# Seeding the expert sums with x, and a differently ordered loop of expert pairs, in a two-layer encoder trunk

## The chip, the cores and the metric

The kernel runs on one core of a Trainium2 chip. The metric is the device time in microseconds (us), as the median over runs; lower is better. The engines are TensorE (PE in the profile; PEld is its weight loads), VectorE (DVE), ScalarE (ACT), GpSimd (POOL) and SyncE (SP), which here issues nearly all DMA transfers.

## The reference, cut to what matters

The input x has 256 tokens of 1024 channels. There are two layers, each a mixer followed by a mixture of experts; the end is an RMS norm. The change touches only the mixture's sum and the end.

```python
def hier_moe(...):            # 4 groups of 8 experts; top-1 group, top-2 experts in it
    ...
    hg = jnp.einsum('sd,edf->sef', t, w_gate)      # 32 experts, 1024 -> 256
    hu = jnp.einsum('sd,edf->sef', t, w_up)
    act = jax.nn.silu(hg) * hu * combine[:, :, None]
    return jnp.einsum('sef,efd->sd', act, w_down)  # 256 -> 1024

for i in range(2):
    x = x + g_m * mixer_i(modulate(rmsnorm(x)))
    x = x + g_f * hier_moe(modulate(rmsnorm(x)))
return rmsnorm(x, norm_out)
```

All data are float32. The weights of 32 experts in each of two layers (3 MB an expert) are most of what is read from memory.

## The kernel before, in words

Each engine has its own program, and semaphores order them. The work around the change is `experts(l)`, which exists once for each engine, for layer l = 0 and 1.

**Pairs of experts.** The kernel routes the 512 token copies (256 tokens, two experts each) so that the copies of one expert stand together, and takes the experts two at a time: 16 pairs p = 0 to 15 in a layer. Each expert has a window of 64 slots; the two windows of a pair make the 128 rows of one tile. Two pairs make a group, `group(i)`, with b = p % 2 naming the buffer of a pair. (With badly unbalanced routing there would be more groups; the number is read from a register, and is 8 here.)

**TensorE, for pair p:** `gate_half` (32 matmuls, L983), `up_half` (L995), `turn_act` (two transposes of the activations, L1003), and then `down` of the pair *before* it, p - 1 (L1016). `combine(p - 2)` (L1042) multiplies the result of pair p - 2 by a 0/1 matrix `sel` and so adds each slot's row to its token's row: eight matmuls, on four PSUM banks (bank 4 and 5 for the first 512 columns of the two token tiles, 6 and 7 for the second). The result is carried as a high and a low float32r part, hence `part`. The banks 4 to 7 gather the sum over all pairs of a layer.

**Where combine stands before the change:** for p = 2 and 3 behind `up_half`; from p = 4 on between `gate_half` and `up_half`. Groups 0 and 1 are written out, and the loop `Fori(2, groups)` does the rest. The very first matmuls on the banks (p = 0) start the sum with start=True. After the loop come `down_last` (L1028) for pair 15 and the combines of the pairs 14 and 15, the last of which raise `mix_done`.

**VectorE, for pair p:** `silu_mul` (the product that turns gate and up into the activation, L1776 and L1781), `places` (L1788 to L1795: it builds `sel` for pair p, and waits for the semaphore `comb_done`, since combine(p - 2) reads the same buffer), `keep_y(p - 1)` (L1806 evacuates `down`, L1811 makes the low part). **ScalarE:** the windows of the next pair, tanh, the copy of the turned activations, and the high part (`high_y`, L1310). Both have loops of their own, which start at group 2.

**SyncE** issues the weight loads in one order of its own, in one queue: gate(p), up(p) (2 MB each, L348 and L352), and down (2 MB, L356 and L361). gate(p) waits for `gate_done` of pair p - 2, up(p) for `unit_done` of pair p - 2 (the last matmul of `up_half`), down for `down_done`. So a transfer can be issued when TensorE has finished with the slot two pairs before, and not earlier; a wait holds all that is behind it in this program. The last down weights come as four transfers of 0.5 MB (L431).

**After the experts:** `combined(l)` on VectorE adds the four banks to x_res (L1849), in the order first half, both tiles, second half, both tiles; ScalarE squares what has been added (`squares`, L1139) with a running sum; VectorE turns the sums into mean squares (`mean_square`, L1381 and L1383) and GpSimd takes the power -1/2 (`power`, L474). At the very end this is spread over two tiles: VectorE multiplies x by the norm's gain (L1876), GpSimd takes two powers (L550), ScalarE scales tile 0 (L1362), VectorE does tile 1 in one instruction of 1024 columns (L1880), and SyncE stores the tiles (L446) as each is done.

## Time and profile before

| | |
|---|---|
| time, median of 3 runs | 685.51 us (684.13 to 686.7) |
| time of the profiled execution | 686.04 us |
| span of the profiled execution | 684.3 us |
| PE busy | 628.0 us (92%) |
| DVE busy | 358.6 us (52%) |
| ACT busy | 179.4 us (26%) |
| read from memory | 268.17 MB, 393 GB/s over the span |

A span is shorter than its execution's time by what lies around it, 1.7 us here. Busy times are sums over stages with different limits: TensorE at 92% and the queue of weight loads (96.6% of the 16 DMA engines' span) both look full, and which of them sets the time has to be read stage by stage. A row of the timeline has its start, its length, engine and line, the operation with its tiles, how many instructions were merged (x32), and in brackets the idle time before it with what ended it.

### The profile page before, as it was taken

How to read it: one execution, taken by the hardware profiler on the slowest of the kernel's cores; microseconds unless marked ns; L12 is line 12 of the kernel's file. 1: busy time of each engine (PE TensorE's matmuls, PEld its weight loads, DVE VectorE, ACT ScalarE, POOL GpSimd, SP SyncE). 2: the span in 40 equal slices, each digit the busy share in tenths (PEclk: the TensorE clock that was granted, in tenths of full speed). 3: DMA queues.
4: the chain of work that ended last, by engine and by line, in shares of the span. 5: the costliest groups of instructions: out<-in, count | busy, mean ns of one | idle time of the engine just before them, and what ended most of it. 6: DMA issues, size and time to landing. Idle time of an engine off the chain costs nothing.

```text
span 684.3 us, 11449 instructions
## 1 busy us (share of the span) xinstructions
PE 628.0 (92%) x4226; PEld 378.8 (55%) x4226; DVE 358.6 (52%) x869; ACT 179.4 (26%) x370; POOL 62.3 (9%) x111
## 2 busy tenths in 40 slices
PE   2799999998999999999998989999999999999894
PEld 1597758446766455545554457666555544555442
DVE  2257988998454643344334465735444344433445
ACT  2123252013431222122212233342223122221213
POOL 5010408950000000000000000000000000000000
PEclk9899999999999999999999999999999999999998
DMA  8999967999999999999999999999999999999991
GB/s 326 367 399 394 381 249 269 400 417 417 383 410 418 422 420 422 421 423 422 423 421 421 408 399 411 420 420 422 421 420 420 422 421 421 422 421 423 422 375 65
DMA packets 51534, 269.63 MB, mean 394 GB/s; under 512 B 4112, under 2 KB 6224, under 8 KB 27440
## 3 DMA queue, kind: packets, MB, share of 16 engines
q1 hardware_dynamic: 50720, 268.22, 96.6%
q0 software_dynamic: 784, 1.01, 0.5%
q8 instruction: 19, 0.31, 0.2%
q14 instruction: 11, 0.09, 0.0%
HBM read 268.17 MB, written 1.05 MB: 393 GB/s over the span
## 4 chain that ended last, share of the span: by engine, by line
PE 75%; DMA 17%; DVE 5%; issue 1%; SPq 0%; ACT 0%; POOL 0%; DVEq 0%; POOLq 0%
PE bank L983 15%; PE bank L995 14%; PE bank L1016 12%; DMA ring<-in_w_gate 11%; PE bank L1042 7%; DMA ring<-in_w_mod 6%; PE bank L860 4%; PE bank L699 4%; PE bank L948 2%; PE bank L783 2%; PE bank L793 2%; DVE hT L1781 2%; PE bank L612 2%; PE bank L1003 1%; PE bank L729 1%
## 5 line engine op out<-in xcount | busy, mean ns | idle before, releaser
L983 PE MATMUL bank<-ring,arena 128*64 128x256 f32 x1024 | 116.9, 380 | 3.5 <-DMA ring<-in_w_gate 3.5
L995 PE MATMUL bank<-ring,arena 128*64 128x256 f32 x1024 | 117.2, 381 | 0.0
L983 PEld LDWEIGHTS bank<-ring,arena 128*64 128x64 f32 x1024 | 75.6, 137 | 51.8 <-issue 21.6
L995 PEld LDWEIGHTS bank<-ring,arena 128*64 128x64 f32 x1024 | 72.3, 137 | 41.1 <-issue 8.6
L1781 DVE SCALAR_TENSOR_TENSOR hT<-hT,bank 128x256 f32<-128x256 f32 x32 | 19.2, 602 | 136.6 <-PE bank L995 136.6
L1310 ACT CAST xn_parts<-arena 128x512 fp32r<-128x512 f32 x64 | 39.6, 619 | 106.8 <-DVE arena L1806 106.8
L1806 DVE SCALAR_TENSOR_TENSOR arena<-bank,hT,gates 128x512 f32<-128x512 f32 x64 | 48.0, 750 | 36.7 <-PE bank L1016 35.4
L1042 PE MATMUL bank<-xn_parts,sel 128*128 128x512 f32 x256 | 67.1, 405 | 0.0
L1016 PE MATMUL bank<-dn_w,hT 128*64 128x512 f32 x256 | 58.5, 598 | 1.1 <-ACT gates L1120 1.1
L1042 PEld LDWEIGHTS bank<-xn_parts,sel 128*128 128x128 f32 x256 | 45.7, 188 | 20.9 <-issue 12.4
L1016 PE MATMUL bank<-xn,arena 128*64 128x512 f32 x112 | 51.1, 598 | 0.0
L1016 PE MATMUL bank<-gates,arena 128*64 128x512 f32 x112 | 51.1, 598 | 0.0
L1776 DVE SCALAR_TENSOR_TENSOR hT<-hT,bank 128x256 f32<-128x256 f32 x32 | 13.5, 421 | 64.1 <-ACT hT L1297 64.0
L1811 DVE TENSOR_TENSOR xn_parts<-arena,xn_parts 128x512 fp32r<-128x512 f32 x64 | 44.0, 687 | 2.8
L1290 ACT COPY arena<-arena 128x512 f32 x64 | 39.9, 623 | 9.6 <-issue 6.1
L1016 PEld LDWEIGHTS bank<-dn_w,hT 128*64 128x64 f32 x256 | 17.3, 136 | 30.9 <-issue 30.9
L612 PE MATMUL bank<-ring,cs 128*32 128x256 f32 x288 | 19.6, 421 | 14.6 <-DMA ring<-in_w_mod 14.6
L1003 PE MATMUL bank<-ident,hT 128*128 128x128 f32 x64 | 13.7, 295 | 19.3 <-DVE hT L1781 19.3
L1463 DVE SCALAR_TENSOR_TENSOR gates<-ring,cs,gates 128x1024 f32<-128x1024 f32 x23 | 30.1, 1308 | 0.8
L1301 ACT COPY hT<-bank 128x256 f32<-128x256 f32 x16 | 6.0, 372 | 92.6 <-PE bank L1003 92.6
L1301 ACT COPY arena<-bank 128x256 f32<-128x256 f32 x16 | 6.0, 373 | 88.1 <-PE bank L1003 88.1
L1016 PEld LDWEIGHTS bank<-xn,arena 128*64 128x64 f32 x112 | 14.2, 136 | 26.3 <-issue 26.3
(326 smaller groups left out, 768.0 us busy)
## 6 DMA issues: line engine op xcount, KB each, us to landing
ring<-in_w_gate SPq DMA_DIRECT2D x32, 2048.0 KB, 18.3
ring<-in_w_up SPq DMA_DIRECT2D x32, 2048.0 KB, 18.8
ring<-in_w_mod SPq DMA_DIRECT2D x20, 2048.0 KB, 17.5
dn_w<-in_w_down SPq DMA_DIRECT2D x16, 2048.0 KB, 18.3
xn<-in_w_down SPq DMA_DIRECT2D x14, 1024.0 KB, 16.9
gates<-in_w_down SPq DMA_DIRECT2D x14, 1024.0 KB, 19.8
ring<-in_w_in SPq DMA_DIRECT2D x2, 2048.0 KB, 22.0
dn_w<-in_w_mod SPq DMA_DIRECT2D x2, 2048.0 KB, 12.0
```

Source lines behind the costliest of these rows:

```text
L612: ins = pe.matmul(quadrant(vec, q), cs[:, 2, k:k + 1].to_broadcast([P, 32]), by_quadrant(w[:, kk, :], q, natural), start=not last and kk = ...
L699: ins = pe.matmul(bank[banks[m // 2]][:, (m % 2) * T:(m % 2 + 1) * T], w[:, k, m * P:(m + 1) * P], hT[:, k, :], start=(k == 0), stop=(k == ...
L983: ins = pe.matmul(bank[2][h * WIN:(h + 1) * WIN, 0:FE], xw[:, b, h, k, :], w[:, h, 0, k, :], start=(k == 0), stop=(k == KT - 1))
L995: ins = pe.matmul(bank[3][h * WIN:(h + 1) * WIN, 0:FE], xw[:, b, h, k, :], w[:, h, 1, k, :], start=(k == 0), stop=(k == KT - 1))
L1016: ins = pe.matmul(bank[n][h * WIN:(h + 1) * WIN, :], actT[b][:, t, h * WIN:(h + 1) * WIN], w[h][:, t, n * HALF:(n + 1) * HALF], start=(t = ...
L1042: ins = pe.matmul(bank[4 + 2 * n + t][:, :], sel[:, b, t * P:(t + 1) * P], xn_parts[:, part, b, n * HALF:(n + 1) * HALF], start=(isinstanc ...
L1290: ins = act.copy(xw[:, b, h], xgT[:, :, bass.ds(start, WIN)])
L1310: act.copy(xn_parts[:, 0, b, at], y_s[:, b, at]).then_inc(e["y_hi"], 1)
L1463: ins = stt(acc, w, cs[:, 2, k:k + 1], acc, ALU.mult, ALU.add)
L1781: stt(act_s.rearrange("s t p -> s p t"), gl.rearrange("s (p t) -> s p t", t=FT), 0.5, bank[3][:, 0:FE].rearrange("s (p t) -> s p t", t=FT) ...
L1806: stt(y_s[:, b, at], bank[n][:, :], slot_gate[:, b:b + 1], gates[:, 2 * l + 1, at], ALU.mult, ALU.mult).then_inc(e["y_kept"], 1)
L1811: tt(xn_parts[:, 1, b, at], y_s[:, b, at], xn_parts[:, 0, b, at].bitcast(F32), ALU.subtract).then_inc(e["y_lo"], 1)
```

## The change: what it does

- `start_with_x()`, new: behind group 0, TensorE multiplies the identity by x_res (float32), four products of 128x512, with start=True on the banks 4 to 7. So the expert sums begin with x, and no matmul of combine has start=True any more.
- `combine` takes a list of halves. For every pair from p = 2 on, the first half (banks 4 and 5) stands between `gate_half` and `up_half`, the second (banks 6 and 7) between `up_half` and `turn_act`. `comb_done` comes with the second.
- TensorE's loop starts at group 1. The loops of the other engines are as before.
- `combined(0)` copies the banks to x_res where it added them. `combined(1)` is gone.
- At the end ScalarE squares the banks themselves, once `mix_done` says that each is complete; VectorE multiplies the first halves (banks 4, 5) by the gain after the square of the same bank, then `mean_square(4)`, one `power(4)` for both tiles; VectorE finishes the second halves from the banks 6, 7, ScalarE scales the first halves, and SyncE stores tile t when both halves are done.

```diff
@@ SyncE, the stores
             for t in range(TT):
-                sp.wait_ge(*((S["x_scaled"], 3), (S["out_dve"], 1))[t])
+                sp.wait_ge(S["out_act"], t + 1)
+                sp.wait_ge(S["out_dve"], t + 1)
@@ GpSimd
-            for t in range(TT):
-                pool.wait_ge(S["mean_sq"], 5 + t)
-                pool.tensor_tensor(stat[:, 4 + t:5 + t], stat[:, 2 + t:3 + t], mhalf[:, 0:1], ALU.pow).then_inc(S["inv_rms"], 1)
+            power(4)
@@ TensorE, experts
-                def combine(p, b, last=False):
-
-                    if isinstance(p, int) and p == 0:
-                        pe.wait_ge(S["rows_act"], l + 1)
-                        pe.wait_ge(S["rows_dve"], l + 1)
+                def start_with_x():
+
+                    pe.wait_ge(S["rows_act"], l + 1)
+                    pe.wait_ge(S["rows_dve"], l + 1)
+                    for half in range(2):
+                        for t in range(TT):
+                            pe.matmul(bank[4 + 2 * half + t][:, :], ident[:], x_res[:, t, half * HALF:(half + 1) * HALF], start=True, stop=False)
+
+                def combine(p, b, halves=(0, 1), last=False):
+
                     pe.wait_ge(e["sel_kept"], p + 1)
-                    for n in range(2):
+                    for n in halves:
                         pe.wait_ge(e["y_lo"], p * 2 + (n + 1))
...
-                                                start=(isinstance(p, int) and p == 0 and part == 0), stop=(last and part == 1))
+                                                start=False, stop=(last and part == 1))
                             if last:
                                 ins.then_inc(S["mix_done"], 1)
-                    if not last:
+                    if not last and n == 1:
                         ins.then_inc(e["comb_done"], 1)
@@ group(i)
                         gate_half(p, b, i * 16 + 16)
-                        if n == XS:
-                            combine(p - 2, b)
+                        if n >= 2:
+                            combine(p - 2, b, (0,))
                         up_half(p, b, i * 16 + 16)
+                        if n >= 2:
+                            combine(p - 2, b, (1,))
...
-                        if 2 <= n < XS:
-                            combine(p - 2, b)
                         turn_act(p)
...
                 group(0)
-                group(1)
-                with pe.Fori(2, groups) as i:
+                start_with_x()
+                with pe.Fori(1, groups) as i:
                     group(i)
@@ ScalarE, squares and the end
                         else:
-                            act.wait_ge(S["x_ready" if half else "x_half"], TT * (n - 1) + t + 1)
+                            act.wait_ge(S["mix_done"], 10 + 2 * half + t + 1)
...
+                        x_now = x_res[:, t, at] if n < 4 else bank[4 + 2 * half + t][:, :]
...
-            act.wait_ge(S["x_scaled"], 2)
             act.wait_ge(S["inv_rms"], 5)
-            act.activation(xn[:, 0, :], xn[:, 0, :], ACT.Identity, scale=stat[:, 4:5]).then_inc(S["x_scaled"], 1)
+            for t in range(TT):
+                act.wait_ge(S["x_scaled"], t + 1)
+                act.activation(xn[:, t, 0:HALF], xn[:, t, 0:HALF], ACT.Identity, scale=stat[:, 4 + t:5 + t]).then_inc(S["out_act"], 1)
@@ VectorE, combined and the end
-                    ins = tt(x_res[:, t, at], x_res[:, t, at], bank[4 + i][:, :], ALU.add)
+                    ins = dve.tensor_copy(x_res[:, t, at], bank[4 + i][:, :])
...
-            combined(1)
-            dve.wait_ge(S["square_sum"], 2 * TT * 4 + TT)
-            done(ts(stat[:, 0:2], stat[:, 20:22], 1.0 / D, EPS, ALU.mult, ALU.add))
             dve.wait_ge(S["row_kept"], 2)
             for t in range(TT):
-                at = slice(t * HALF, (t + 1) * HALF)
-                tt(xn[:, 0, at], x_res[:, 0, at], gates[:, 0, at], ALU.mult).then_inc(S["x_scaled"], 1)
-                dve.wait_ge(S["square_sum"], 2 * TT * 4 + TT + t + 1)
-                stt(stat[:, 2 + t:3 + t], stat[:, 22 + t:23 + t], 1.0 / D, stat[:, t:t + 1], ALU.mult, ALU.add).then_inc(S["mean_sq"], 1)
-            dve.wait_ge(S["inv_rms"], 6)
-            stt(xn[:, 1, :], x_res[:, 1, :], stat[:, 5:6], gates[:, 0, :], ALU.mult, ALU.mult).then_inc(S["out_dve"], 1)
+                dve.wait_ge(S["square_sum"], 2 * TT * 4 + t + 1)
+                tt(xn[:, t, 0:HALF], bank[4 + t][:, :], gates[:, 0, 0:HALF], ALU.mult).then_inc(S["x_scaled"], 1)
+            mean_square(4)
+            dve.wait_ge(S["inv_rms"], 5)
+            for t in range(TT):
+                stt(xn[:, t, HALF:D], bank[6 + t][:, :], stat[:, 4 + t:5 + t], gates[:, 0, HALF:D], ALU.mult, ALU.mult).then_inc(S["out_dve"], 1)
```

## Rows read from the trace of the kernel before

**Rows 1.** The page, part 2: rate of all transfers in 40 slices of 17.1 us.

```profile
GB/s 326 367 399 394 381 249 269 400 417 417 383 410 418 422 420 422 421 423 422 423 421 421 408 399 411 420 420 422 421 420 420 422 421 421 422 421 423 422 375 65
```

**Rows 2.** TensorE's timeline: start us, length us, what; gate of pair 15, both layers.

```profile
379.82 3.67 PE L983 MATMUL bank<-ring,arena 128*64 128x256 f32 x32 [0.81 <-DMA ring<-in_w_gate]
...
654.04 3.67 PE L983 MATMUL bank<-ring,arena 128*64 128x256 f32 x32 [0.81 <-DMA ring<-in_w_gate]
```

**Rows 3.** TensorE's timeline: pair 9 of layer 1, in the loop.

```profile
567.73 3.62 PE L983 MATMUL bank<-ring,arena 128*64 128x256 f32 x32
571.28 2.11 PE L1042 MATMUL bank<-xn_parts,sel 128*128 128x512 f32 x8
573.32 3.67 PE L995 MATMUL bank<-ring,arena 128*64 128x256 f32 x32
577.76 0.44 PE L1003 MATMUL bank<-ident,hT 128*128 128x128 f32 x2 [0.76 <-DVE hT L1781]
...
581.61 3.62 PE L983 MATMUL bank<-ring,arena 128*64 128x256 f32 x32
```

**Rows 4.** TensorE's timeline: gates of pairs 3 and 4, layer 0.

```profile
212.87 3.62 PE L983 MATMUL bank<-ring,arena 128*64 128x256 f32 x32
...
225.64 3.62 PE L983 MATMUL bank<-ring,arena 128*64 128x256 f32 x32
```

**Rows 5.** TensorE's timeline: two float32 products of 128x512.

```profile
193.97 1.88 PE L629 MATMUL bank<-gates,ones 128*128 128x512 f32 x4
```

**Rows 6.** SyncE's timeline: issues of single 2 MB weight loads.

```profile
180.46 0.38 SPq L348 DMA_DIRECT2D ring<-in_w_gate  x1
...
203.91 0.40 SPq L348 DMA_DIRECT2D ring<-in_w_gate  x1
...
476.58 0.40 SPq L348 DMA_DIRECT2D ring<-in_w_gate  x1
...
633.56 0.38 SPq L352 DMA_DIRECT2D ring<-in_w_up  x1
638.50 0.37 SPq L356 DMA_DIRECT2D dn_w<-in_w_down  x1
```

**Rows 7.** DMA view, one issue each, order of rows 6: last column us to landing.

```profile
ring<-in_w_gate SPq DMA_DIRECT2D x1, 2048.0 KB, 7.7
...
ring<-in_w_gate SPq DMA_DIRECT2D x1, 2048.0 KB, 11.7
...
ring<-in_w_gate SPq DMA_DIRECT2D x1, 2048.0 KB, 11.9
...
ring<-in_w_up SPq DMA_DIRECT2D x1, 2048.0 KB, 25.2
...
dn_w<-in_w_down SPq DMA_DIRECT2D x1, 2048.0 KB, 25.3
```

**Rows 8.** Windows of 5 us: last columns granted clock, DMA share, GB/s.

```profile
180.00:185.00 5.00, 4.79 (x46) 2.65 (x42) 1.02 (x2) 0.99 (x3) 0.00 (x0) 1.00 0.84 283
```

**Rows 9.** DMA view of 200 to 204 us: queue, packets, MB, share of 16.

```profile
q8 instruction: 1, 0.02, 1.7%
```

**Rows 10.** Timeline of the end, all engines.

```profile
664.49 3.65 PE L1016 MATMUL bank<-dn_w,hT 128*64 128x512 f32 x16
...
674.13 2.48 DVE L1849 TENSOR_TENSOR x_res<-x_res,bank 128x512 f32<-128x512 f32 x4 [0.37 <-PE bank L1042]
...
676.71 0.61 ACT L1139 ACTIVATE arena<-x_res 128x512 f32<-128x512 f32 x1
...
679.18 1.28 DVE L1880 SCALAR_TENSOR_TENSOR xn<-x_res,stat,gates 128x1024 f32<-128x1024 f32 x1 [0.89 <-POOL stat L550]
679.89 0.96 SPq L446 DMA_DIRECT2D out<-xn  x2
```

**Rows 11.** Timeline behind layer 0: last square to the first user of the power.

```profile
403.01 0.19 ACT L1139 ACTIVATION_READ_ACCUMULATOR arena<-x_res 128x1 f32 x1
...
404.28 1.42 DVE L1390 TENSOR_SCALAR xn<-x_res,stat 128x1024 f32<-128x1024 f32 x2 [0.81 <-POOL stat L474]
```

More of the change, by code:

```diff
@@ L279, in trunk @@
             slot_ready sel_ready rows_turned rows_act rows_dve xg_done xg_act xg_dve xw_half win_ready
-            row_done row_kept band_ready x_scaled out_dve out_stored scale_ready dve_own pool_own""".split()
+            row_done row_kept band_ready x_scaled out_act out_dve out_stored scale_ready dve_own pool_own""".split()
         S = {n: sem(n) for n in names}
@@ L1135, in squares @@
                             act.wait_ge(S["x_in"], 16 * TT)
+                        elif n < 4:
+                            act.wait_ge(S["x_ready" if half else "x_half"], TT * (n - 1) + t + 1)
                         else:
-                            act.wait_ge(S["x_ready" if half else "x_half"], TT * (n - 1) + t + 1)
+                            act.wait_ge(S["mix_done"], 10 + 2 * half + t + 1)
                         at = slice(half * HALF, (half + 1) * HALF)
-                        act.activation(ar((9216 if n else 0) + t * D + half * HALF, HALF), x_res[:, t, at], ACT.Square,
+                        x_now = x_res[:, t, at] if n < 4 else bank[4 + 2 * half + t][:, :]
+                        act.activation(ar((9216 if n else 0) + t * D + half * HALF, HALF), x_now, ACT.Square,
                                        accum_out=stat[:, 20 + 2 * half + t:21 + 2 * half + t]).then_inc(S["square_sum"], 1)
```

## The prediction, made before the changed kernel was run

> **What bounds the kernel now.** I read the page's rates first. From the tenth slice on, through both loops, the transfers run at 417 to 423 GB/s nearly without a break [rows 1]; that is a full queue, and the reader is to see that it does not dip where the loops run. Then TensorE's timeline. In the middle of a layer it never waits for a transfer: a pair in the loop takes 13.88 us (567.73 to 581.61) and its only idle time is 0.76 us ahead of the transposes, where VectorE's product is awaited [rows 3]. A pair needs 6 MB of weights, three transfers of 2,097 KB, which at 421 GB/s take 4.98 us each, 14.9 a pair. So TensorE is faster than its weights by 1.06 us a pair, and eats up the lead that it got while the layer was being routed. Late in each layer the lead is gone: the gates of the last pairs (14 and 15 in layer 0, 13 to 15 in layer 1) wait for their transfer, 0.81 us at the gate of pair 15 in both layers [rows 2]. So the time at which pair 15 can start is that of a landing, and it is the end of a queue that has run without a gap since the layer's beginning. Both engines look full, but the queue binds: what TensorE saves in the loop, it will wait for at the end of the loop. What counts is (a) whether the landings move, and (b) the path from the last gate's landing, just ahead of 654.04, to the end of the span, 684.3.
>
> **The change, part by part.** *x opens the sums:* four float32 products of 128x512. Two take 1.88 us with their drain [rows 5], four some 3.5, once in each layer, behind group 0. They delay everything of pair 2 and 3 on TensorE by 3.5 us. *The loop:* the pairs 2 and 3 had their combine behind `up_half` already, and pair 3 takes 12.77 us (212.87 to 225.64) against 13.88 [rows 4, 3]: eight matmuls behind `up_half` hide VectorE's product. Now half of them stand there, 2.04 / 2 = 1.0 us (the whole takes 571.28 to 573.32), against an idle time of 0.76: covered, with 0.25 to spare. Splitting it adds two changes between the two kinds of matmul; no row has their price alone. I take 0.17 for both, an estimate between 0 and 0.3 (gate's 32 matmuls take 3.55 us ahead of combine, so little is lost at the change there [rows 3]), so 12.95 us a pair. That is 0.93 us less for each of the 12 pairs of the loop, 11 a layer, of which the x products take 3.5, and the queue takes the rest: TensorE now meets the landings from about pair 11 or 12 on and waits 2.0 us at each. `comb_done` comes half a combine later, so `places` starts some 0.5 us later; behind it on VectorE stands `keep_y(p - 1)`, and this stands as it does in pair 3 now, where TensorE shows no wait: nothing. *The loop from group 1 on:* no instruction more; pairs at the loop's turn take as long as the others; nothing, except the fetch of instructions, below. *`combined(0)`:* a copy for an add of the same tile, and ahead of a TensorE that waits for weights there: nothing.
>
> **(a) Do the landings move?** gate(4) is issued when the gate of pair 2 is done, so 3.5 us later: 207.4 for 203.91 in layer 0, 480.1 for 476.58 in layer 1 [rows 6]. There the queue is at its shortest. The price of a late issue is bounded from both sides. In layer 0 gate(2) was issued at 180.46 to a queue that had just run dry: it landed 7.7 us later, and the window around it fell to 283 GB/s, (419 - 283) / 419 x 5 = 1.6 us of the queue's time [rows 6 to 8]. By the landing: 207.4 + 7.7 = 215.1 is no later than the 203.91 + 11.7 = 215.6 of now, and in layer 1 480.1 + 7.7 = 487.8 against 488.5 [rows 6, 7]. So gate(4) has 0.5 and 0.7 us of slack even if it meets an empty queue; up(4), issued 4.6 us later than now, is still issued over 3 us before gate(4) lands. That bound says 0. By the rate: the total rate would dip in both places as it did at 180, at most 1.6 us each, 3.2 in all. The two disagree since a landing is that of the slowest of 16 engines: gate(4) needs 11.7 us though the queue ahead of it holds little more than one transfer, so one engine lags behind the mean, and the others' dip costs nothing. Below zero: an instruction fetch holds one engine for 1.7% of 16 x 4 us = 1.1 us [rows 9], and TensorE's program is shorter by one group in each layer; a fetch fewer on the lagging engine brings the landings forward by 1.1 us a layer at most, 2.2 in all. I take 0, the landings' own bound, and keep +3.2 and -2.2 for the range.
>
> The Trainium skill (DMA: Bandwidth & Descriptors, "Why a DMA increments its semaphore by 16 and not by 1") says that the engines of a transfer finish independently and only the full 16 means that all has landed. By that rule the landing's bound counts, and not the mean rate's; the trace agrees in that gate(4) of layer 0 takes 11.7 us behind a short queue [rows 7]. The same page ("Anatomy of one DMA") fits a transfer by 2.0 us plus its bytes at 436 GB/s, for another issuing path; by that 2 MB take an estimated 6.8 us where the row has 7.7, gate(4) would land at 214.2, and the sum would still be 0.
>
> **(b) The end.** Now the down of pair 14 starts at 664.49 [rows 10], 10.45 us behind the gate of pair 15 [rows 2]. In the new order that is 12.95 less down (577.76 to 581.61 less 0.36 of transposes, 3.49 [rows 3]), 9.5, so 663.5 if no weights are late. But up(15) landed at 633.56 + 25.2 = 658.8 and down(14) at 638.50 + 25.3 = 663.8 [rows 6, 7]; I allow 0.25 from a landing to the first matmul, an estimate. So `up_half` starts at 659.05 for 658.7, down at 664.1. TensorE gains 0.4 us, not 0.9; what is late next is the weights again. From there to the last product nothing changes, so VectorE's first add of now, at 674.13, is at 673.7 only a semaphore.
>
> Then: four squares of 0.61 from the banks, the first at 673.75 instead of 0.7 behind an add; the last starts at 675.6 and, with its accumulator read, ends at 676.3. Now the last starts at 676.71 and ends at 677.4 [rows 10]. VectorE's two products (about 0.7 each) lie between the squares. From the end of the last square to the first user of the power behind layer 0 it is 403.20 to 404.28, 1.08 us, with one power for both tiles [rows 11]: the last stage starts at 677.4. Now it starts at 679.18, since two powers run one after the other [rows 10]. Two products of 512 columns instead of one of 1024 columns, 0.75 and then 0.7 (1.28 now): done at 678.1 and 678.85, against 680.46. The stores: now the first is issued at 679.89 and the second right behind VectorE's end, and the span ends 3.84 behind that end; the first store is ready at 678.15 and doesn't hold the second. 678.85 + 3.84 = 682.7: the end gains 1.6 us, 0.4 of it on TensorE. Where the skipped add lets the squares start, the banks' readers are ordered one behind the other; if ScalarE reads a bank slower than x_res, at most 0.1 a square, it costs 0.4; if `up_half` were not held by its landing, it gains 0.5 more.
>
> **Sum.** Landings 0, end -1.6: the profiled execution goes from 686.04 to 684.4, span 682.7. This execution stood 0.5 above the median of its kernel, so 684.1 between the two.
>
> **Rivals.**
> *The late issues cost the queue (slower):* the fourth gate transfer of each layer, issued 3.5 us later, meets a dry queue, and the dip passes on to every landing behind it: 2 x 1.6 - 1.6 = +1.6, 687.6. For it: the rate fell to 283 GB/s in the like case [rows 8], and nothing later in a layer can give it back. Against: the landing's slack of 0.5 and 0.7 us. It turns into a slower kernel when the two dips cost over 1.6 together.
> *Fewer fetches (faster):* the queue's slowest engine is spared one instruction fetch in each layer; 2.2 + 1.6 = 3.8 less, 682.2. For it: the program is shorter, and a fetch stands in the stretch of the late landings [rows 9]. Against: in layer 0 gate(4) can't land before 215.1, which leaves 0.5 to gain there.
> *TensorE's saving shows:* 2 x (11 - 3.5) = 15 less, near 670. For it: TensorE is the busier engine and stands on most of the chain. Against: the waits for weights at pair 15 in both layers [rows 2]; for it the queue would have to be faster than 421 GB/s, which no slice shows [rows 1].
> *The half doesn't cover:* the transposes still wait. It would show in a pair over 13.2 us, and cost nothing but the 0.4 at the end: 684.8, since the queue binds.
>
> **Numbers.** Forecast (with the fourth rival, which can't be told from it in the time) 0.68, late issues 0.17, fewer fetches 0.13, TensorE's saving 0.02. Range 682.0 to 687.6: it reaches to both neighbours. Half a per cent, about what a measurement can tell from no change here, is 3.4 us: faster means below 682.1. Of the fewer fetches nearly all but the full case stays above that, so faster 0.09; slower, above 688.9, needs dips over twice as dear as the rows have them, 0.04; within 0.87.
>
> **What would show it.** Right: gate of pair 15 starts within 1 us of 379.8 and 654.0, waiting about 2 us for its transfer, in both layers; waits of that kind from pair 11 or 12 on; a pair in between of 12.9 to 13.0 us with no idle time ahead of L1003; 8 instructions of 3.5 us behind group 0; up of pair 15 held by its landing; span's end some 28.7 us behind the last gate for 30.3. Wrong: gates of pair 15 later by over 1 us with a dip near 207 or 480 (late issues), or earlier by over 1 (fetches); pairs without waits at a layer's end (TensorE's saving); or an end that doesn't shrink, say for a slower read of the banks.

## The result, and the profile after

The changed kernel takes 687.63 us (median of 17 runs, 684.93 to 693.97), the kernel before 684.55 beside it (17 runs, 683.51 to 687.47). The ratio is 1.0052, 95% interval 1.0034 to 1.0070: slower by about 3 us. The forecast was 684.1, a small gain.

The profiled execution of after took 685.28 us (span 683.5), 2.3 below the median of its kernel, so it can show only part of the loss. Its span is even 0.8 shorter than that of before, since layer 0's loads start 1.6 us earlier in it (gate(2) is issued at 178.87 for 180.46 [rows 6]), ahead of anything that the change touches. So stretches are compared, each from its own start, and a second profile of the same kernel (e1 below, 687.55 us, at its median) stands beside it.

The page of after, part 2 (rate of all transfers, 40 slices) and part 3 (queues: packets, MB, share of 16 engines):

```profile
GB/s 329 366 394 394 375 298 256 413 417 417 382 415 347 425 421 422 422 422 422 422 422 422 409 399 410 420 419 420 364 424 421 422 421 421 422 422 422 422 413 117
...
q1 hardware_dynamic: 50720, 268.22, 97.0%
...
q8 instruction: 16, 0.26, 0.2%
```

Where [rows 1] run level, two slices now dip, the 13th (418 before, 347 after) and the 29th (421 before, 364 after). They are the places of gate(4), the load of the gate weights of pair 4, in the two layers.

Windows of 5 us, two of before and then those of after (last columns: granted clock, DMA share, GB/s):

```profile
203.00:208.00 5.00, 5.00 (x44) 3.72 (x41) 1.04 (x2) 0.38 (x1) 0.00 (x0) 1.00 0.99 392
480.00:485.00 5.00, 5.00 (x24) 2.52 (x25) 3.40 (x9) 0.50 (x2) 0.00 (x0) 1.00 1.01 416
...
203.00:208.00 5.00, 5.00 (x42) 3.08 (x40) 0.42 (x1) 0.38 (x1) 0.00 (x0) 1.00 0.76 269
208.00:213.00 5.00, 5.00 (x38) 2.92 (x36) 1.77 (x5) 0.37 (x1) 0.00 (x0) 1.00 0.98 395
213.00:218.00 5.00, 5.00 (x37) 2.44 (x34) 3.74 (x8) 1.90 (x4) 0.00 (x0) 1.00 0.99 374
480.00:485.00 5.00, 5.00 (x42) 3.06 (x40) 0.42 (x1) 0.38 (x1) 0.00 (x0) 1.00 0.83 310
```

The first dip in windows of 1 us of after:

```profile
205.00:206.00 1.00, 1.00 (x11) 0.47 (x8) 0.00 (x0) 0.03 (x1) 0.00 (x0) 1.00 0.69 279
206.00:207.00 1.00, 1.00 (x6) 0.55 (x6) 0.42 (x1) 0.35 (x1) 0.00 (x0) 1.00 0.17 74
207.00:208.00 1.00, 1.00 (x11) 0.71 (x12) 0.00 (x0) 0.00 (x0) 0.00 (x0) 1.00 0.95 156
208.00:209.00 1.00, 1.00 (x14) 0.64 (x12) 0.00 (x0) 0.00 (x0) 0.00 (x0) 1.00 0.88 295
```

SyncE's timeline of after, around pair 4 (issues; layer 0, then layer 1):

```profile
178.87 0.38 SPq L348 DMA_DIRECT2D ring<-in_w_gate  x1
...
206.12 0.41 SPq L348 DMA_DIRECT2D ring<-in_w_gate  x1
210.69 0.38 SPq L352 DMA_DIRECT2D ring<-in_w_up  x1
...
481.48 0.41 SPq L348 DMA_DIRECT2D ring<-in_w_gate  x1
```

DMA view of after, one issue each: gate(4), up(4) of layer 0, gate(4) of layer 1; last column is us from issue to landing:

```profile
ring<-in_w_gate SPq DMA_DIRECT2D x1, 2048.0 KB, 8.1
...
ring<-in_w_up SPq DMA_DIRECT2D x1, 2048.0 KB, 10.9
...
ring<-in_w_gate SPq DMA_DIRECT2D x1, 2048.0 KB, 8.0
```

From gate(2)'s issue to gate(4)'s it is 27.25 us now (206.12 - 178.87), 23.45 before [rows 6]: 3.8 later. gate(4) takes 8.1 us to land for 11.7 [rows 7], which is close to what a transfer takes on a queue that has run dry (7.7). up(4) lands at 210.69 + 10.9 = 221.6, which is 7.4 us behind gate(4) and not the 5.0 of a full queue. The same up(4) in before, its issue and its DMA view:

```profile
207.21 0.38 SPq L352 DMA_DIRECT2D ring<-in_w_up  x1
...
ring<-in_w_up SPq DMA_DIRECT2D x1, 2048.0 KB, 13.3
```

TensorE's timeline of after: the products of x, a pair, and the gates of pairs 12 and 15 (layer 0), pair 15 (layer 1):

```profile
198.62 3.70 PE L1037 MATMUL bank<-x_res,ident 128*128 128x512 f32 x8
202.25 3.67 PE L982 MATMUL bank<-ring,arena 128*64 128x256 f32 x32
...
228.53 3.62 PE L982 MATMUL bank<-ring,arena 128*64 128x256 f32 x32
232.08 1.20 PE L1046 MATMUL bank<-xn_parts,sel 128*128 128x512 f32 x4
233.21 3.67 PE L994 MATMUL bank<-ring,arena 128*64 128x256 f32 x32
236.81 1.21 PE L1046 MATMUL bank<-xn_parts,sel 128*128 128x512 f32 x4
237.86 0.38 PE L1002 MATMUL bank<-ident,hT 128*128 128x128 f32 x2
...
241.66 3.62 PE L982 MATMUL bank<-ring,arena 128*64 128x256 f32 x32
...
336.14 3.67 PE L982 MATMUL bank<-ring,arena 128*64 128x256 f32 x32 [1.47 <-DMA ring<-in_w_gate]
...
380.83 3.67 PE L982 MATMUL bank<-ring,arena 128*64 128x256 f32 x32 [1.43 <-DMA ring<-in_w_gate]
...
655.29 3.67 PE L982 MATMUL bank<-ring,arena 128*64 128x256 f32 x32 [1.44 <-DMA ring<-in_w_gate]
```

A pair takes 13.13 us (228.53 to 241.66) with nothing idle ahead of the transposes, and in layer 0 five gates (pairs 11 to 15) and in layer 1 four (12 to 15) wait for their weights. TensorE has become faster than its weights by what was forecast; only the weights come later. From gate(2)'s issue to the start of pair 15, layer 0 takes 380.83 - 178.87 = 201.96 us for 379.82 - 180.46 = 199.36 [rows 2, 6]: 2.6 later.

The end of after, all engines:

```profile
674.82 0.60 ACT L1146 ACTIVATE arena<-bank 128x512 f32<-128x512 f32 x1 [1.08 <-PE bank L1046]
...
677.02 0.22 ACT L1146 ACTIVATION_READ_ACCUMULATOR arena<-bank 128x1 f32 x1
...
677.59 0.69 POOL L475 TENSOR_TENSOR stat<-stat,mhalf 128x2 f32<-128x2 f32 x1 [248.98 <-DVE stat L1391]
...
678.32 1.41 DVE L1885 SCALAR_TENSOR_TENSOR xn<-bank,stat,gates 128x512 f32<-128x512 f32 x2 [0.80 <-POOL stat L475]
679.14 1.02 SPq L447 DMA_DIRECT2D out<-xn  x2
```

From the start of pair 15 it is 683.5 - 655.29 = 28.2 us to the span's end, for 30.3 before [rows 2]: the end gained 2.0.

### The profile page after: what moved, and what is told of

Same layout as the page of the kernel before. It is cut to its first block, busy times and chain, and to the rows that moved or that the text cites. A ratio compares the mean times of both kernels' runs of the same rounds, so it can differ in the third digit from the quotient of the medians.

```text
span 683.5 us, 11501 instructions
## 1 busy us (share of the span) xinstructions
PE 636.9 (93%) x4242; PEld 378.4 (55%) x4242; DVE 358.5 (52%) x865; ACT 179.2 (26%) x371; POOL 62.8 (9%) x110
## 4 chain that ended last, share of the span: by engine, by line
PE 43%; issue 37%; DMA 17%; DVE 2%; SPq 0%; ACT 0%; POOLq 0%; DVEq 0%; POOL 0%
DMA ring<-in_w_gate 11%; PE bank L982 7%; DMA ring<-in_w_mod 6%; PE bank L994 5%; PE bank L1015 4%; PE bank L859 4%; PE bank L698 4%; PE bank L1046 2%; PE bank L782 2%; PE bank L792 2%; PE bank L611 2%; PE bank L947 1%; PE bank L1103 1%; PE bank L745 1%; PE bank L728 1%
## 5 line engine op out<-in xcount | busy, mean ns | idle before, releaser
L982 PE MATMUL bank<-ring,arena 128*64 128x256 f32 x1024 | 117.1, 380 | 12.1 <-DMA ring<-in_w_gate 12.1
L1046 PE MATMUL bank<-xn_parts,sel 128*128 128x512 f32 x256 | 75.1, 419 | 0.0
L1046 PEld LDWEIGHTS bank<-xn_parts,sel 128*128 128x128 f32 x256 | 43.5, 188 | 29.4 <-issue 23.2
L475 POOL TENSOR_TENSOR stat<-stat,mhalf 128x2 f32<-128x2 f32 x5 | 3.5, 702 | 531.4 <-DVE stat L1391 531.4
## 6 DMA issues: line engine op xcount, KB each, us to landing
dn_w<-in_w_mod SPq DMA_DIRECT2D x2, 2048.0 KB, 11.7
```

What stands on the lines that cost most here:

```text
L982: ins = pe.matmul(bank[2][h * WIN:(h + 1) * WIN, 0:FE], xw[:, b, h, k, :], w[:, h, 0, k, :], start=(k == 0), stop=(k == KT - 1))
L1046: ins = pe.matmul(bank[4 + 2 * n + t][:, :], sel[:, b, t * P:(t + 1) * P], xn_parts[:, part, b, n * HALF:(n + 1) * HALF], start=False, sto ...
```

## The experiments

Times are medians with the range. Each set has its own runs of the kernel before: 685.25 us for e1 to e4, 685.92 for e5 to e8, 685.81 for e9 to e11, 684.96 for e12. For the traces one table serves all, three stretches read from TensorE's and SyncE's timelines as above: in layer 0 from gate(2)'s issue to the start of pair 15; and from the products with the second half of the weights that layer 1's mixer waits for (L600, L601 before) to gate(2)'s issue in layer 1, and to the start of pair 15 in layer 1.

```
kernel (profiled execution)       layer 0    to gate(2)   layer 1
before                            199.36     47.85        248.78
after                             201.96     47.84        248.90
e1  after again                   201.01     49.48        250.28
e2  x behind the gate of pair 2   200.92     50.21        251.07
e4  before's order of combine     201.72     48.64        250.37
e6  after, filled middle          201.63     48.64        250.15
e5  x in pair 3                   199.25     50.14        248.74
e11 e5 again                      199.49     50.29        248.84
e7  e5, filled middle             199.30     47.84        248.14
e12 e5, idle products in pair 5   199.61     50.26        249.90
e8  split order alone             198.21     50.11        248.56
e9  before, idle x ahead          201.69     47.84        249.56
e10 before, idle x behind up      201.37     48.54        249.92
```

One execution's row is good to about a microsecond: e8's layer 0 reads 1.2 us under before's, though its kernel issues nothing earlier behind gate(2).

**e1: the changed kernel again.**

> The changed kernel itself, to see the spread of its runs and their granted clocks side by side. Theory 1 (clock): TensorE now waits for weights at the gates of the last four or five pairs of each layer, and in some runs its clock is lowered to half in that stretch; the time then goes up as the mean granted clock goes down: runs from 685 (clock 0.998) to 693 (0.982), median near 687.5, while the kernel before stays within 3 us at 684.5. Theory 2 (late issues): gate(4) of each layer comes late and every run pays the same, some 1.5 to 3 us net; then the runs would lie together and the clock would not matter.

687.6 us (685.41 to 694.18, 12 runs), ratio 1.0039 (1.0016 to 1.0063): the loss holds. Windows of its trace:

```profile
203.00:208.00 5.00, 5.00 (x38) 2.88 (x36) 0.42 (x1) 0.38 (x1) 0.00 (x0) 1.00 0.84 326
208.00:213.00 5.00, 5.00 (x39) 3.16 (x38) 0.68 (x2) 0.00 (x0) 0.00 (x0) 1.00 0.97 331
480.00:485.00 5.00, 5.00 (x39) 3.04 (x40) 0.42 (x1) 0.38 (x1) 0.00 (x0) 1.00 0.80 326
485.00:490.00 5.00, 5.00 (x40) 3.21 (x40) 0.90 (x3) 0.10 (x1) 0.00 (x0) 1.00 1.00 357
```

The same dips, and layer 1 is late here too, by 1.5 us (250.28). Of the two theories the expectation names, the mean clock (0.983 to 0.995) does go with the time here, and the late issues are in the trace; the runs of e1 alone don't part them.

**e2: the products behind the gate of pair 2**, so that gate(4) need not wait for them.

```diff
                         gate_half(p, b, i * 16 + 16)
+                        if n == 2:
+                            start_with_x()
...
-                start_with_x()
-                with pe.Fori(1, groups) as i:
+                group(1)
+                with pe.Fori(2, groups) as i:
```

> The four x products stand behind the gate matmuls of pair 2 in place of ahead of them (so pairs 2 and 3 are written out again), so gate(4) is issued as early as in the kernel before. Theory 2 (late issues): the dip of the transfer rate near 207 and 480 us goes, the lowest run falls by 1.5 to 3 us against the changed kernel's, to about 682.5. Theory 1 (clock): the lowest falls by that too if the dips cost anything, but the waits at the last gates get no shorter, so the upper runs stay 5 us and more above the lowest and the median stays above the lowest by 2 us or more.

688.27 us (685.64 to 690.11), ratio 1.0034 (1.0017 to 1.0051): nothing gained, and the lowest run is 685.64, not the 682.5 that both theories expected. gate(4) was issued at 204.87, but up(4), whose wait is for the last matmul of `up_half`, 8.0 us later at 212.88; the dips stood at 213 to 223 (297 and 333 GB/s). The late issue had only been moved from one transfer to the next; my expectation looked at gate(4) alone.

**e3: idle products in each pair of the loop**, three of 128x256 in float32 ahead of the wait for the gate's weights, whose result nothing reads: is it TensorE's idle time, with the clock behind it, that costs?

```diff
                         pe.wait_ge(e["gl_ready"], p)
+                        if not isinstance(p, int):
+                            for _ in range(3):
+                                pe.matmul(bank[2][:, FE:2 * FE], ident[:], slot_no[:, 0:FE], start=True, stop=True)
+                        pe.wait_ge(gate_in[l][b], loaded)
```

> In each pair from 2 on, three idle float32 products of 128x256 (1.3 us in all, result not used) stand ahead of the wait for the gate's weights. TensorE does more work and waits less. Theory 1 (clock): the spread goes, every run has a granted clock of 0.99 or more, and the median falls to 685 to 686, under the changed kernel's although 30 x 1.3 = 39 us of work is added. Theory 2: the median stays at 687.5; and if TensorE were the bound it would rise by up to 39 us.

714.85 us (714.09 to 715.04), ratio 1.0421 (1.0395 to 1.0446). TensorE's timeline, a pair of its layer 1:

```profile
580.29 1.56 PE L979 MATMUL bank<-slot_no,ident 128*128 128x256 f32 x6
581.78 3.67 PE L986 MATMUL bank<-ring,arena 128*64 128x256 f32 x32
```

The filler took 1.56 us a pair, in 14 pairs of each layer, and a pair 14.77. That is 21.8 us a layer, and TensorE's waits for gate weights in after, which could hide it, are 12.1 us in both layers together (its page). The experiment was ill-sized and says nothing on the clock.

**e4: the order of the combines as before**, x and the end as after; the loop starts at group 2 again.

```diff
-                        if n >= 2:
-                            combine(p - 2, b, (0,))
+                        if n == XS:
+                            combine(p - 2, b)
                         up_half(p, b, i * 16 + 16)
-                        if n >= 2:
-                            combine(p - 2, b, (1,))
...
+                        if 2 <= n < XS:
+                            combine(p - 2, b)
```

> Combine stands as in the kernel before (whole, behind up for pairs 2 and 3, ahead of up from pair 4 on), the loop starts at group 2; x products and the end on the banks as in the changed kernel. Theory 1 (clock): a pair takes 13.9 us again, TensorE reaches the landings only at pair 13 or so and the waits are 0.8 us: no spread, every clock 0.99, median 684.5 + (1.5 to 3 of late issues) - 1.2 of the end = 685 to 686. Theory 2: the same median as the changed kernel less the 0.4 that the split gives at the end, so 688.

686.15 us (685.67 to 689.69), ratio 1.0012 (0.9995 to 1.0029). The dips are there without the new order (270 GB/s at 203 to 208, 324 at 480 to 485). The time is the one expected by the clock theory (685 to 686) and not the 688 of the late issues. But no gate of a pair 15 waits for weights: with pairs as slow as before's, the 3.7 us of products make TensorE itself the bound, so its time can't be set beside after's term by term.

**e5: the products of x in pair 3.** Pair 0's combine starts the sums again; x is added in pair 3 behind its combine, behind everything that releases gate and up of the pairs 4 and 5. The loop starts at group 2, as it does in e2; everything else is the changed kernel.

```diff
-                def start_with_x():
+                def add_x():
...                          start=False, stop=False)
                             combine(p - 2, b, (1,))
+                        if n == 3:
+                            add_x()
...
-                start_with_x()
-                with pe.Fori(1, groups) as i:
+                group(1)
+                with pe.Fori(2, groups) as i:
```

> The changed kernel, but combine of pair 0 starts the sums and the four x products are added in pair 3, behind its combine; so no gate or up transfer is issued late while the queue is short, only down(6), where it is longer. Theory 2 (late issues): the dips near 206 and 482 us (269 and 310 GB/s) go, gate of pair 15 of layer 0 comes 199 to 200 us behind the issue of gate(2) as before, for 201 to 202; the lowest run falls by 1.5 to 2.5 us to about 683, the median by as much. Theory 1 (clock): the wait for the second w_mod weights between the layers stays at 2.2 us and more, so the clock is still lowered there in part of the runs and the median stays 2 us or more above the lowest.

683.16 us (681.64 to 684.50, 12 runs), ratio 0.9967 (0.9954 to 0.9980). It beats the kernel before and, by the ratios, the changed one by 0.7%. Windows of its trace:

```profile
203.00:208.00 5.00, 5.00 (x40) 2.88 (x36) 0.42 (x1) 0.38 (x1) 0.00 (x0) 1.00 0.98 378
208.00:213.00 5.00, 5.00 (x26) 2.25 (x26) 3.47 (x9) 0.99 (x2) 0.00 (x0) 1.00 1.02 429
...
475.00:480.00 5.00, 5.00 (x42) 3.43 (x40) 2.24 (x4) 2.42 (x5) 0.00 (x0) 1.00 0.99 369
480.00:485.00 5.00, 5.00 (x38) 2.96 (x36) 1.50 (x4) 0.37 (x1) 0.00 (x0) 1.00 1.01 416
...
490.00:495.00 5.00, 5.00 (x42) 3.02 (x38) 0.45 (x2) 0.95 (x2) 0.00 (x0) 1.00 1.02 429
```

The two dips are gone (a window of layer 1, 475 to 480, still reads 369 for 419 before, and pair 15 there is not late), and layer 0 is back at 199.25. So the whole loss goes with the place where the change put the products; in pair 3 no cost of them can be told. e2 has the same loop and the same work and keeps the loss, so it isn't the loop's start.

**e6 and e7: a filled wait between the layers.** Three idle float32 products of 128x512 ahead of the wait for the mixer's weights, in the changed kernel (e6) and in e5 (e7): does the loss come from a TensorE that idles there and then runs at the lower clock?

```diff
                     key = halves(vec)[part]
+                    if vec == (1, 2) and part == 1:
+                        for _ in range(3):
+                            pe.matmul(bank[2][:, :], ident[:], slot_no[:], start=True, stop=True)
                     arrived(key)
```

> The changed kernel with three idle float32 products of 128x512 (2.6 us, result not used) ahead of the one wait for weights between the layers (2.3 us in the changed kernel's profile, 3.0 us in its rerun, where the 16 matmuls behind it took 3.58 us in place of 1.92, at half clock). Theory 1: no half clock behind it any more, the mean granted clock rises from 0.990 to 0.993 or more, median 686 or less, time no longer rising to 694. Theory 2: same as the changed kernel, 687.5.

> Both edits: x products in pair 3, and the idle products ahead of the wait between the layers. If the two causes are separate the gains add: median 683.5 to 684.5, under the kernel before's 685.25 by about 1 (the end's 1.6 to 2.0 us are kept, the late issues and the lowered clock are gone). If only the clock matters it equals the one with the filled wait; if only late issues, the one with x in pair 3.

e6: 687.86 us (685.23 to 690.38), ratio 1.0037 (1.0020 to 1.0054). e7: 682.96 (681.24 to 685.09), ratio 0.9967 (0.9950 to 0.9985). In e6 the mean granted clock over all runs rose from 0.990 to 0.994 and the median did not move, and e7 is e5 within 0.2 us. That stretch is not where the loss of the median is. The clock theory may be right about the slowest runs: none of e6's 12 is above 690.4, where 6 of the 29 of after and e1 are (690.5 to 694.2); 12 runs are too few to show it.

**e8: the split order of the combines alone**, in the kernel before (a `combine` that takes halves, one ahead of `up_half` and one behind it).

> The kernel before with the split combine alone (no x products, the old end, the loop from group 2). Theory 1 (clock): TensorE is early at the end of layer 0 and its wait between the layers grows from 1.73 to 2.3 us or more, so the clock is lowered there in part of the runs and the median rises by 1 us or more above the kernel before, to 686 to 687, with no dip at 206 or 482 us. Theory 2 (late issues): nothing is issued late, so it is the kernel before's median less 0.4 at the end, 685.

686.66 us (682.74 to 688.11), ratio 1.0011 (0.9995 to 1.0027): no change that can be told. The new order saves TensorE time and the queue takes it back, as forecast. Its median is in the clock theory's range (686 to 687), above the 685 of the late issues, and its mean clock is the lowest of all (0.987, 0.990 before); so a small loss by the clock is not excluded here.

**e9 and e10: the products alone, thrown away**, in the kernel before; ahead of the gate of pair 2 (e9) or behind `up_half` of pair 2 (e10). The first combine still starts the sums.

```diff
                 group(0)
+                pe.wait_ge(S["rows_act"], l + 1)
+                pe.wait_ge(S["rows_dve"], l + 1)
+                for half in range(2):
+                    for t in range(TT):
+                        pe.matmul(bank[4 + 2 * half + t][:, :], ident[:], x_res[:, t, half * HALF:(half + 1) * HALF], start=True, stop=True)
                 group(1)
```

> The kernel before, with the eight products of x run ahead of the gate of pair 2 in both layers and their result thrown away (the first combine still opens the sums); order of the combines, and the end, as before. Late-issue theory: the transfer rate has its dips of the changed kernel, about 270 GB/s in layer 0 where the gate of pair 4 is loaded (392 before) and about 310 in layer 1, the loads come 1.7 to 2.6 us later in layer 0 and 0.1 to 1.5 in layer 1, and as this kernel has no gain at its end, its time is 2 to 4 us above before: 688 to 690 where before has 685.9. Rival (the sums on the banks, the order of the combines or the new end lose the time, not the place of the products): no more than the 0.7 us or so that TensorE's own lead would lose, 686 to 686.7. Wrong for late issues: a dip as expected and a time within 1 us of before.

> The kernel before with the same eight thrown-away products, but behind the up part of pair 2 and ahead of the first combine, where they are behind both matmul groups that release the loads of pair 4. Late-issue theory: no dip (392 and 416 GB/s as before), the gate of pair 4 issued as before, and a time of before to 1 us above it, 685.9 to 686.9; at least 1.2 us below the kernel that has them ahead of the gate. Rival (3.7 us of TensorE's time cost the same wherever they stand): both kernels with idle products agree within 0.5 us.

e9: 689.38 us (687.29 to 690.55, 6 runs), ratio 1.0055 (1.0037 to 1.0073). e10: 688.76 (687.14 to 690.45, 7 runs), ratio 1.0043 (1.0026 to 1.0059). e9 is where the late issues put it (688 to 690), and above the 686.7 of its rival. But e10 is only 0.6 us below e9, where I expected 1.2 at least and the rival 0.5 at most: by the times the rival is close and mine is missed. The windows say more. e9:

```profile
208.00:213.00 5.00, 5.00 (x43) 3.28 (x40) 1.04 (x2) 0.39 (x1) 0.00 (x0) 1.00 0.73 251
```

e10:

```profile
203.00:208.00 5.00, 5.00 (x42) 3.41 (x38) 1.02 (x2) 0.38 (x1) 0.00 (x0) 1.00 0.98 400
...
218.00:223.00 5.00, 5.00 (x50) 3.25 (x46) 0.98 (x2) 1.63 (x3) 0.00 (x0) 1.00 0.91 334
```

In e9 the products alone make the dip (251 GB/s; gate(4) is issued 27.25 us behind gate(2), as in after, and lands in 7.9); in layer 1 it is small, 383 GB/s at 480 to 485, not the 310 expected. In e10 gate(4) is issued on time (23.46) and its window holds, but the down loads behind it come 3.4 us late and the dip, a smaller one, stands there. In neither does the gate of a pair 15 wait for weights: before, its waits late in layer 0 are down to about a microsecond [rows 2], so 3.7 us more work make TensorE the bound wherever it stands. The two show where a dip comes from; in this kernel their time can't tell the dip from the work.

**e11: e5 again.**

> The changed kernel with the products of x in pair 3 behind its combine, the same kernel as e5_x_in_pair3, beside new runs of before. If the gain found there is the kernel's and not that set of runs: ratio 0.994 to 0.999, 2 to 3.5 us below before. If it was chance: ratio within 0.001 of 1.

684.02 us (682.21 to 685.74, 12 runs), ratio 0.9974 (0.9960 to 0.9989). The gain of e5 holds, at about 2 to 3 us.

**e12: e5 with a second load of about the same size, later**: seven idle products (3.3 us by its trace, 3.6 expected) in pair 5, where TensorE is ahead of its weights and the queue is full. Pairs 4 and 5 are written out.

```diff
+                        if isinstance(p, int) and p == 5:
+                            for _ in range(7):
+                                pe.matmul(bank[2][:, FE:2 * FE], ident[:], slot_no[:, 0:FE], start=True, stop=True)
```

> The kernel with the products of x in pair 3, plus another 3.6 us of idle products of TensorE ahead of the gate of pair 5 in both layers (seven of 128x256, 0.52 us each by the run with idle products; pairs 4 and 5 are written out for it). By pair 5 a load comes some 13 us behind its issue, so an issue 3.6 us late still finds the queue filled; and TensorE has waits of 4.3 us (layer 0) and 4.0 us (layer 1) for landings behind that place. Place theory: the time stays within 1 us of the kernel without them (683.2 and 684.0 in its two sets of runs, 2 to 3 below before), no dip in the transfer rate, and at most one wait for a gate left in each layer. Rival (3.7 us of TensorE cost the same anywhere, as in both kernels with idle products before, which lost 3.0 and 3.6 us): about 3 us above it, at or above the kernel before.

684.22 us (683.04 to 685.24, 12 runs), ratio 0.9987 (0.9976 to 0.9999). By the ratios that is 0.9 to 1.4 us above e11 and e5 for 3.3 us of work in each layer, at or just over the 1 us that the place theory allowed, and not the 3 us of the rival. Two gates still wait in each layer (0.58 and 1.34, 0.61 and 1.32 us), not one, and the rate is a little lower there: slices 14 to 16 read 415, 419 and 418 GB/s (422, 420 and 422 before), slices 30 to 32 of layer 1 read 411, 424 and 415 (420, 422 and 421 before). The microsecond is in layer 1 (249.90 for 248.84), which in this execution also began 2.4 us late (50.26); whether it comes from the small dips or from a lead of TensorE that had to serve both is not shown.

## Why the prediction was wrong, step by step

**What bounds the kernel: right.** The weights set both ends of the loops. The waits at the gates came at pairs 11 to 15 in layer 0 as forecast; TensorE's saving does not show by itself (e8).

**The pair: right, 0.18 off.** 13.13 us for 12.95; four products 3.70 for some 3.5; the half combine covers VectorE's product.

**(b), the end: right.** 2.0 us gained for 1.6. The waits at pair 15 are 1.4 us for the 2.0 forecast.

**(a), "Do the landings move?": this is the step that failed.** It took the landing's bound, "that bound says 0", over the rate's bound of 1.6 us a dip. For gate(4) itself the landing's bound was nearly exact: counted from gate(2)'s issue it landed at 35.35 us for 35.15 before. But the bound was worked out for one transfer, and the next was dismissed in half a sentence (up(4) "is still issued over 3 us before gate(4) lands"). Counted in the same way up(4) landed at 42.72 us for 40.05: 2.7 later, and 2.6 was still missing at pair 15. The time was lost ahead of gate(4), not behind it. Between 206 and 207 us, when gate(4) had just been issued, 0.17 of the engines' time was in use; from 205 to 209 the rate was 279, 74, 156 and 295 GB/s, which at 421 is 2.1 us of the queue's time (in before some 0.7 is missing between 200.6 and 205.6, around the issue of its own gate(4)). At up(4)'s issue they were busy again (393 GB/s at 210 to 211). gate(4)'s landing didn't show that gap, up(4)'s did. That "one engine lags behind the mean, and the others' dip costs nothing" is what was wrong for layer 0: what the dip didn't cost gate(4), it cost the *next* transfer.

In layer 1 of the same execution it held. gate(4) landed as before, up(4) 0.8 us later than before, the two halves of the down load behind it 1.6 and 1.3, and the gate load of pair 5 on time again, 51.4 us behind gate(2)'s issue for 51.5 (494.57 + 11.1 - 454.23, before 489.33 + 15.3 - 453.11). So the price of one dip (310 GB/s at 480 to 485) was nothing there. Which engine lags in either layer no view here shows.

The Trainium skill (DMA: Bandwidth & Descriptors, "Why a DMA increments its semaphore by 16 and not by 1") says that the engines of a transfer finish independently and that only the full 16 means that all has landed. No row shows single engines, and the rule is not contradicted; but it decides only when one transfer counts as landed. I had used it to set the rate's bound aside, and it says nothing of the transfer behind: up(4) came 7.4 us behind gate(4).

**The rival "late issues" was right** in place and in mechanism for layer 0. That its 687.6 is what was measured is partly luck: it was a rise of 1.6 us, counted from an execution of 686.04, and the measured rise is 3.1, from a median of 684.55. It was given 0.17, though the only row of a like case [rows 8] spoke for it, because of a slack read from one landing in each layer.

**What the profile of one execution hid.** Layer 1 shows no loss in the trace of after (248.90), and 1.4 to 1.5 us in those of e1 and e6. The table tells why. In the kernels that hold TensorE up nowhere ahead of pair 3, layer 1 swallows a late start: in e5, e8 and e11 gate(2) is issued 2.3 us later than before, and pair 15 starts on time (248.56 to 248.84); only e12, with its work in pair 5, begins as late and ends 1.1 late. In e1, e2, e4 and e6 it is 0.8 to 2.4 us late and pair 15 is late by 1.4 to 2.3. By these few traces the slack was real, but executions in which TensorE comes late were already living on it, and the products used it up. Over the runs it shows as spread: the changed kernel ranges from 684.9 to 694.2, e5 and e11 from 681.6 to 685.7.

Layer 0 lost 2.6 us and layer 1 0.1 in the trace of after, 1.7 and 1.5 in e1, 2.3 and 1.4 in e6, and the end gave back 2.0: +0.7, +1.2 and +1.7 by these stretches, where the medians of the three say +3.1, +2.4 and +1.9. Part of the difference lies outside these stretches: gate(2) of layer 0 is issued 1.6 us earlier than before in the trace of after and 0.5 earlier in those of e1 and e6, and from pair 15 of layer 0 to the mixer's products it takes 0.1, 0.8 and 0.5 longer. The rest lies in the one execution of before, which stood 1.5 us above its median in the result (686.04 for 684.55), 0.8 above that of e1's set and 0.1 above that of e6's, and in that of after, 2.3 below its own median. The products' place is shown to be the cause, since the same products in pair 3 take the whole of it away. Not settled: the share of each layer in the median, for the profile of after is of one of its shortest executions; and how e5's 2 to 3 us under the kernel before divide, since its end gains 2.0 and e8's order gives nothing by itself.

**"Fewer fetches": no sign of it.** There are 16 instruction fetches for 19 in after, e1 and e6, and they have layer 0 at 201.96, 201.01 and 201.63. e4 and e9, with the same late gate(4) and all 19 fetches, have 201.72 and 201.69, though there TensorE sets the end. So no gain of the forecast size shows; one of some tenths of a microsecond could not be told from the spread of such rows.

## What to carry to other kernels

Ahead of work whose end releases a load, TensorE's time is priced by the queue's depth and not only by TensorE's slack: if issue to landing, less the delay, comes down to the time of a transfer on a dry queue (here 11.7 us less 3.8, against 7.7), the delay can cost, as it did in layer 0 of every trace with a late gate(4), and the same work one pair and a half later costs nothing that could be told. Check not only the delayed load but the one behind it. A slack read from one execution may be what other executions live on, so look at the spread of the runs before spending it. And count a rival's price from the same median as the result.

## What the runs showed of the hardware

**A late transfer can hand its delay on.** In before, gate(4) took 11.7 us from issue to landing, and the window around it read 392 GB/s. Issued 3.8 us late into a short queue it took 8.1, the window fell to 269 GB/s, and the load behind it took 7.4 us from landing to landing for 5.0. In layer 0 the delay of that one, 2.7 us, was not made up in the more than 30 loads behind it, which ran at about 422 GB/s; in layer 1 a delay of 0.8 to 1.6 us was gone by the gate load of pair 5.

**The granted clock goes with the spread.** TensorE ran at the lower of its two levels (1.2 GHz) for part of some windows, and where differs from execution to execution: the mean of 5 us is 0.67 at 165 to 170 and 0.72 at 405 to 410 in e1, and in before 0.75 at 35 to 40. TensorE's timeline of e1, products with weights that it had waited for:

```profile
407.27 3.58 PE L600 MATMUL bank<-ring,cs 128*32 128x512 f32 x16 [3.01 <-DMA ring<-in_w_mod]
```

and of e5, where the same products ran at 2.4 GHz:

```profile
404.80 1.92 PE L600 MATMUL bank<-ring,cs 128*32 128x512 f32 x16 [2.17 <-DMA ring<-in_w_mod]
```

The 1.66 us between the two are as much as e1's gate(2) of layer 1 comes late by the table (49.48 for 47.85).

Taking each run's time at the lower level from its mean clock c as (1 - c) x 2 x span, a straight line through the 17 runs of after rises by 0.40 us for each us at the lower level (correlation 0.91; granted clock 0.998 goes with 684.9 to 685.4 us, 0.982 with 693.4), through those of e1 by 0.37, of the sets of before by 0.14 to 0.22, of e5 by 0.10 and e11 by 0.20. That a kernel whose loads have slack hides more of such a stretch would fit, but the lines don't part cleanly: e7, with the products in pair 3, has 0.23, and e2, with the loss, 0.24. It is a correlation over runs, and no cause is shown by it; e6 raised the mean clock without any gain in the median.
